# Split of the weights in pairs of K tiles, all products with the high half ahead of those with the low half, and stationary tiles on multiples of 64 bytes

## The chip, the cores and the metric

The kernel runs on one core of one Trainium2 chip. The metric is the device time of one execution in microseconds (us), the median of the runs shown. The core has five engines that run at the same time, each through its own queue in order, and wait for one another by semaphores: PE (TensorE, matmuls), DVE (VectorE), ACT (ScalarE), POOL (GpSimd) and SP (SyncE, which here only issues the loads). Weights come from HBM by DMA into SBUF; matmuls add into PSUM banks of 512 fp32 columns.

## The reference

Everything is fp32. 256 rows of 2048 columns pass through two transformer blocks. The first has an adaptive modulation (silu(c) @ w_ada, 2048 x 12288), a differential attention of 8 heads and a latent attention of 8 heads, an output projection and a squared-relu feed-forward of width 8192. The second has three attentions (sliding window, forgetting, memory) whose outputs are gated. Cut to the products that matter here:

```
mod  = silu(c) @ w_ada + b_ada                      # one row: done on DVE, not on PE
proj = modulate(rmsnorm(x)) @ w_in
x    = x + gate_m * (concat(o_diff, o_mla) @ w_out)
f    = square(relu(modulate(rmsnorm(x)) @ w_ff1)) @ w_ff2
x    = rmsnorm(x + gate_f * f)
proj = rms_norm(x) @ w_in_2                         # queries, keys, values, gates
y    = g0 * (ya @ w_a) + g1 * (yb @ w_b) + g2 * (yc @ w_c)
out  = x + y @ w_out_2
```

## The kernel before

**The products.** Every weight product is one "unit": 256 rows times K tiles of 128, into n output columns (n is 512 mostly, else 384, 320, 268 or 256). The activations are the stationary operand, 128 x 128, and the weights are the moving one, 128 x n. To keep fp32 precision each operand is split into a high half of type fp32r and a low half, the rest: for the weights `whi` is a copy of `raw` and `wlo` is `raw - whi`. Each product then is three matmuls: high times high (L324), activations high times weights low (L325), activations low times weights high (L326). A pair of K tiles needs 2 (K tiles) x 2 (row halves t) x 3 = 12 matmuls, in the order of these lines, K tile by K tile. The stationary tiles are called lhsA (attention inputs, first feed-forward product, the second block's input), lhsF (second feed-forward product), lhsM (memory), yz (branch products) and lhsY (last product); each has a `_hi` and a `_lo` half of 16,384 bytes a partition.

**The weights' way.** `plan` is the list of all loads in order, each with two K tiles (512 KB at n = 512), of kind "w" (weights for PE) or "a" and "spare" (pieces of w_ada, which DVE multiplies and adds at L493, or ACT at L491). SP loads them into `raw`, 4 slots, by `load_to` (L211); slot j % 4 is free when the split of load j-4 is done. `consume` (L221) splits one load: for each of its two K tiles one copy on ACT (L234) and one subtraction on DVE (L235), each of n columns, into one of NSPLIT = 7 slots of `whi` and `wlo`. A slot is taken again when the last matmul that reads it (L326 for t = 1) is done.

**The order.** `run` (L296) writes one unit. Ahead of the matmuls of load j, `consume_to(ahead_of(j))` puts the splits up to the second next weight load on the queues of ACT and DVE, and the pieces of w_ada between them. Then come the 12 matmuls, then `pump`, which lets the background generators in `bg` put one step each: attention heads (`causal_head`, `softmax_pv`, `diff_head`), transposes (L379), norms. So each queue holds, in turn, a split, background steps, a split, and so on. The order is fixed when the program is written; only semaphores move things in time. A background step often has work on ACT or DVE that PE waits for in the same step: in `causal_head` DVE writes `lb` (L1363), which the matmul at L1370 reads.

**The memory.** Tensors of SBUF lie one behind another in the order in which they are made, rounded to 32 bytes. `cst` has 1320 columns of 4 bytes, 5280 bytes, which is 82.5 times 64, and `vec` 173 columns, 692 bytes, rounded to 704 (11 times 64). lhsA, `raw`, `whi` and `wlo` lie ahead of `cst` and start at multiples of 64 bytes. All that is made after `cst` starts 32 bytes past one: lhsM, lhsF, yz and lhsY among it.

Of the kernel before, what the change touches and what calls it, by code (L numbers as in the profile page):

```python
# [8 lines left out]
F32 = mybir.dt.float32  # L9
F32R = mybir.dt.float32r  # L10
I32 = mybir.dt.int32
ALU = mybir.AluOpType
ACT = mybir.ActivationFunctionType
AX = mybir.AxisListType.X

P = 128
D = 2048
EPS = 1e-6
LAM0 = 0.8 - 0.6 * float(np.exp(-0.0))
NRAW, NSPLIT = 4, 7  # L20
MAGIC = 12582912.0
RSEED = float(0x5F3759DF)
TWO_PI = (6.28125, 1.93500518798828125e-3, 3.0199160510240e-7)
PI_CLAMP = 3.1415925


C_ID, C_ONE, C_U, C_REL, C_MASK, C_INV, C_END = 0, 128, 256, 512, 896, 1280, 1320

V_SHM, V_SCM, V_SHF, V_SCF, V_GM, V_GF, V_N2, V_MN = [16 * i for i in range(8)]
V_C, V_QA, V_KVA, V_SUB, V_QGA, V_KGA, V_QGB, V_KGB, V_QGC, V_KGC, V_GG, V_END = (  # L30
    128, 144, 148, 150, 151, 152, 153, 154, 155, 156, 157, 173)
# [62 lines left out]
def build(nc, ctx, a, out):  # L94
    def sb(name, shape, dt=F32, scope=ctx):
        return scope.enter_context(nc.sbuf_tensor(name, shape, dt))
# [4 lines left out]
    PE, AC, DV, PO = (Queue(sem(f"s_{n}")) for n in ("pe", "act", "dve", "pool"))  # L101
# [4 lines left out]
    lhsA = Lhs(sb("lhsA_hi", [P, 16, 256], F32R), sb("lhsA_lo", [P, 16, 256], F32R), 16)  # L106
    rows = [Bank(sb(f"row{i}", [P, 2, 512])) for i in range(3)]
    raw = sb("raw", [P, NRAW, 1024])
    whi = sb("whi", [P, NSPLIT, 512], F32R)
    wlo = sb("wlo", [P, NSPLIT, 512], F32R)  # L110
    probs = [Bank(sb(f"probs{i}", [P, 4, 256])) for i in range(2)]
    pts = [Bank(sb(f"pt{i}", [P, 512])) for i in range(2)]
    tmps = [Bank(sb(f"tmp{i}", [P, 512])) for i in range(2)]
    cst = sb("cst", [P, C_END])
    vec = sb("vec", [P, V_END])
    mods = sb("mods", [P, 64])
    small = sb("small", [P, 640])
    mkT = sb("mkT", [P, 4, 256])
# [6 lines left out]
    G = [ctx.enter_context(nc.psum_tensor(f"g{i}", [P, 512], F32)) for i in range(4)]  # L125
    gfree = [[], []]
# [81 lines left out]
    state = dict(load=0, split=0, nsplit=0, unit=0)  # L208
    landed, halves, read, side_loads = {}, {}, {}, {}
# [11 lines left out]
    def consume():  # L221

        j = state["split"]
        kind, _, n, what = plan[j]
        load_to(j + NRAW)
        src = raw[:, j % NRAW, 0:2 * n]
        if kind == "w":
            parts = []
            for kk in range(2):
                s = state["nsplit"]  # L230
                state["nsplit"] += 1
                free = read[s - NSPLIT] if s >= NSPLIT else []
                x, hi, lo = src[:, kk * n:kk * n + n], whi[:, s % NSPLIT, 0:n], wlo[:, s % NSPLIT, 0:n]
                t_hi = AC.put(lambda e, x=x, hi=hi: e.activation(hi, x, ACT.Copy), landed[j], free)  # L234
                t_lo = DV.put(lambda e, x=x, hi=hi, lo=lo: e.tensor_tensor(lo, x, hi.bitcast(F32), ALU.subtract),  # L235
                              landed[j], t_hi, free)
                parts.append((s, hi, lo, t_lo))
            halves[j] = parts
            raw_free[j % NRAW] = [t_lo]
        else:  # L240
            raw_free[j % NRAW] = [ada_part(src, landed[j], *what)]
        state["split"] += 1
        if sums_due and j >= sums_due[0][0]:
            ada_reduce(*sums_due.popleft()[1])
        load_to(j + 1 + NRAW)
# [50 lines left out]
    def run(u, steps=1, width=2):  # L296

        par = state["unit"] % 2
        state["unit"] += 1
        lhs, n, K = u["lhs"], u["n"], u["K"]  # L300
        for b in GB[2 * par:2 * par + 2]:
            while b.busy:
                pump(1, 4)
            gfree[par] = gfree[par] + b.free
            b.free = []
        for i, j in enumerate(u["tiles"]):
            while state["split"] < j and plan[state["split"]][0] == "spare":
                consume()
                pump(1, 6)
            consume_to(ahead_of(j))  # L310
            pair = u["pairs"][i] + u["k_off"] // 2
            while lhs.ready[pair] is None:
                pump(1, 3)
            for kk in range(2):
                k = 2 * i + kk
                ka = 2 * pair + kk
                s, h, l, t_lo = halves[j][kk]
                for t in range(2):
                    o = G[2 * par + t][:, 0:n]
                    xh = lhs.hi[:, ka, t * P:t * P + P]  # L320
                    xl = lhs.lo[:, ka, t * P:t * P + P]
                    first, last = k == 0, k == K - 1
                    w = [t_lo, lhs.ready[pair]] + (gfree[par] if first else [])
                    PE.put(lambda e, o=o, x=xh, w=h, f=first: e.matmul(o, x, w, start=f, stop=False), w, mark=False)  # L324
                    PE.put(lambda e, o=o, x=xh, w=l: e.matmul(o, x, w, start=False, stop=False), mark=False)  # L325
                    tok = PE.put(lambda e, o=o, x=xl, w=h, f=last: e.matmul(o, x, w, start=False, stop=f),  # L326
                                 mark=t == 1)
                read[s] = [tok]
            pump(steps, width)
        u["tok"], u["par"] = tok, par  # L330
        lhs.free = [tok]
        return par, tok
# [142 lines left out]
    start = ExitStack()  # L475
# [72 lines left out]
    k = ready_c["vec"] = t_cols  # L548
# [140 lines left out]
    par, tok = run(u_mem[0], width=3)  # L689
# [7 lines left out]
    par, tok = run(u_mem[1])  # L697
# [343 lines left out]
    for i in range(6):  # L1041
        par, tok = run(u_h0[i], width=3)
# [617 lines left out]
```

How the kernel before makes its waits and increments, by code:

```python
    def run(self, eng):  # L60
        seen = {}
        for waits, fn, sem, by in self.items:
            for s, v in waits:
                if v > seen.get(id(s), 0):
                    eng.wait_ge(s, v)
                    seen[id(s)] = v
            ins = fn(eng)
            if sem is not None:
                ins.then_inc(sem, by)
# [1516 lines left out]
    @block.sync  # L1586
    def _(eng):
        SP.run(eng)
        eng.wait_ge(*t_out)
```

## Time and profile before

| | us |
|---|---|
| median of 3 runs | 2256.26 |
| lowest and highest run | 2246.44, 2257.49 |
| profiled execution, span from first to last instruction | 2249.4 |
| PE busy in it | 2028.9 |
| DVE busy | 1452.0 |
| ACT busy | 1061.2 |
| POOL busy | 215.8 |

The profiled execution is told by its span; the profile has no time for what lies around it. Busy time is the time in which at least one instruction of the engine is in flight. Matmuls are pipelined: one of 512 columns is in flight for 0.39 us while the next has already started, so a busy PE says nothing of its pace, and the pace is read from start to start. The stages lie thus in the span: memory keys and values to 126 us, the first block's input and attention and its output projection to the first feed-forward result at 682, the feed-forward to 1405, the second block's input and attention to the first gate at 1807, gates and branches to 2154, the last product to the end. Pieces of w_ada are used among the weights up to 764 us.

### The profile page before, as it was taken

To read this page: it belongs to the slowest core of one execution; us is meant where nothing else is said; L and a number is where in the kernel's file an instruction comes from. 1 tells how busy PE (TensorE), PEld (TensorE's weight loads), DVE (VectorE), ACT (ScalarE), POOL (GpSimd) and SP (SyncE) were. 2 spreads that over 40 slices of the span, in tenths; PEclk is the share of its full clock that TensorE was granted. 3 is DMA by queue.
4 is the path that set the end of the run, shared out by engine and by line. 5 is a ranking of instruction groups with operands and counts; after the bars stand their busy time and mean duration, and the time that the engine had idled before them with its cause. 6 is when DMAs were issued, how large, how long until landed. Compare 5 with 4: busy or idle time off the path is not lost. (4 is left out here: it accounts for less than half of the span.)

```text
span 2249.4 us, 26960 instructions
## 1 busy us (share of the span) xinstructions
PE 2028.9 (90%) x9432; PEld 1673.3 (74%) x9432; DVE 1452.0 (65%) x2623; ACT 1061.2 (47%) x2120; POOL 215.8 (10%) x247
## 2 busy tenths in 40 slices
PE   5568868977869899999999999988999999999999
PEld 4456656755657688888888887977988887888877
DVE  6887787767778765555555555667666655556544
ACT  3444434553454444544544554545545454444443
POOL 0020043300100010011011012020001001001000
PEclk9788988987999999999999999998999999999999
DMA  8779877636868856555556555643554456666654
GB/s 301 239 248 295 284 262 251 229 94 220 281 234 297 270 178 199 182 189 186 188 173 202 183 181 191 195 117 106 152 148 144 121 162 200 182 196 186 189 188 158
DMA packets 239209, 450.01 MB, mean 200 GB/s; under 512 B 14304, under 2 KB 45280, under 8 KB 238432
## 3 DMA queue, kind: packets, MB, share of 16 engines
q1 hardware_dynamic: 236096, 435.84, 60.5%
q0 software_dynamic: 1856, 9.44, 1.2%
q10 hardware_dynamic: 1120, 3.01, 0.4%
q8 instruction: 74, 1.21, 0.2%
q14 instruction: 63, 0.52, 0.1%
HBM read 444.03 MB, written 4.19 MB: 199 GB/s over the span
## 5 line engine op out<-in xcount | busy, mean ns | idle before, releaser
L235 DVE TENSOR_TENSOR wlo<-raw,whi 128x512 fp32r<-128x512 f32 (+4 forms) x1336 | 896.2, 705 | 516.8 <-ACT whi L234 491.8
L234 ACT ACTIVATE whi<-raw 128x512 fp32r<-128x512 f32 (+4 forms) x1336 | 772.9, 605 | 779.0 <-PE g L326 470.8
L324 PE MATMUL g<-whi,lhsA_hi 128*128 128x512 f32 (+4 forms) x1840 | 716.3, 389 | 43.4 <-DVE wlo L235 34.3
L326 PE MATMUL g<-whi,lhsA_lo 128*128 128x512 f32 (+4 forms) x1840 | 695.0, 378 | 0.0
L325 PE MATMUL g<-wlo,lhsA_hi 128*128 128x512 f32 (+4 forms) x1840 | 694.5, 377 | 0.0
L324 PEld LDWEIGHTS g<-whi,lhsA_hi 128*128 128x128 f32 x1840 | 353.7, 192 | 116.2 <-DVE wlo L235 49.8
L326 PEld LDWEIGHTS g<-whi,lhsA_lo 128*128 128x128 f32 x1840 | 352.3, 191 | 56.9
L325 PEld LDWEIGHTS g<-wlo,lhsA_hi 128*128 128x128 f32 x1840 | 353.7, 192 | 52.4 <-issue 1.2
L493 DVE SCALAR_TENSOR_TENSOR acc<-raw,small,acc 128x512 f32<-128x512 f32 x360 | 278.7, 774 | 37.6 <-DMA raw<-in_w_ada 14.6
L324 PE MATMUL g<-whi,lhsF_hi 128*128 128x512 f32 x512 | 203.8, 398 | 1.1 <-DVE wlo L235 1.1
L325 PE MATMUL g<-wlo,lhsF_hi 128*128 128x512 f32 x512 | 202.2, 395 | 0.0
L326 PE MATMUL g<-whi,lhsF_lo 128*128 128x512 f32 x512 | 202.1, 395 | 0.0
L1113 POOL TENSOR_TENSOR region<-region,tmp 128x512 f32<-128x512 f32 x40 | 57.0, 1444 | 770.4 <-DVE tmp L1109 759.5
L324 PEld LDWEIGHTS g<-whi,lhsF_hi 128*128 128x128 f32 x512 | 96.0, 187 | 24.5 <-DVE wlo L235 1.5
L326 PEld LDWEIGHTS g<-whi,lhsF_lo 128*128 128x128 f32 x512 | 96.0, 187 | 23.5
L325 PEld LDWEIGHTS g<-wlo,lhsF_hi 128*128 128x128 f32 x512 | 96.0, 188 | 23.0 <-issue 0.2
L762 POOL TENSOR_TENSOR rot<-row,trig 128x64 f32<-128x64 f32 (+1 forms) x72 | 37.7, 552 | 231.0 <-ACT row L387 186.3
L517 PE MATMUL pT<-cst,acc 128*128 128x1 f32 x128 | 21.8, 291 | 37.5 <-DVE acc L493 37.5
L1109 DVE TENSOR_TENSOR tmp<-g,region 128x512 f32<-128x512 f32 x40 | 25.8, 686 | 45.9 <-PE g L326 45.9
L517 PEld LDWEIGHTS pT<-cst,acc 128*128 128x128 f32 x128 | 21.6, 251 | 41.5 <-DVE acc L493 40.4
L324 PE MATMUL g<-whi,lhsY_hi 128*128 128x512 f32 x128 | 51.1, 399 | 0.0
L324 PE MATMUL g<-whi,lhsM_hi 128*128 128x512 f32 x64 | 32.0, 501 | 20.9 <-DVE wlo L235 11.5
(291 smaller groups left out, 1690.2 us busy)
## 6 DMA issues: line engine op xcount, KB each, us to landing
raw<-in_w_ff SPq DMA_DIRECT2D x256, 512.0 KB, 4.3
raw<-in_w_ada SPq DMA_DIRECT2D x192, 512.0 KB, 4.8
raw<-in_w_in SPq DMA_DIRECT2D x176, 512.0 KB, 4.4
raw<-in_w_out SPq DMA_DIRECT2D x64, 512.0 KB, 4.7
raw<-in_w_in SPq DMA_DIRECT2D x80, 384.0 KB, 3.6
raw<-in_w_mem_kv SPq DMA_DIRECT2D x16, 512.0 KB, 5.4
raw<-in_w_branch_a SPq DMA_DIRECT2D x12, 512.0 KB, 4.1
raw<-in_w_branch_b SPq DMA_DIRECT2D x12, 512.0 KB, 3.9
```

Source lines behind the costliest of these rows:

```text
L234: t_hi = AC.put(lambda e, x=x, hi=hi: e.activation(hi, x, ACT.Copy), landed[j], free)
L235: t_lo = DV.put(lambda e, x=x, hi=hi, lo=lo: e.tensor_tensor(lo, x, hi.bitcast(F32), ALU.subtract), landed[j], t_hi, free)
L324: PE.put(lambda e, o=o, x=xh, w=h, f=first: e.matmul(o, x, w, start=f, stop=False), w, mark=False)
L325: PE.put(lambda e, o=o, x=xh, w=l: e.matmul(o, x, w, start=False, stop=False), mark=False)
L326: tok = PE.put(lambda e, o=o, x=xl, w=h, f=last: e.matmul(o, x, w, start=False, stop=f), mark=t == 1)
L493: t = DV.put(lambda e, w=w, s=s: e.scalar_tensor_tensor(out=o, in0=w, scalar=s, in1=o, op0=ALU.mult, op1=ALU.add), t_in, b.tok)
L517: tok = PE.put(lambda e, m=m: e.matmul(T.ap[:, m:m + 1], b.ap[:, P * m:P * m + P], ones[:, 0:1], start=True, stop=True), b.tok, T.free, t_cst)
L762: ks = [PO.put(lambda e, o=o, i0=i0, i1=i1: e.tensor_tensor(o, i0, i1, ALU.mult), *w) for o, i0, i1 in ((r[0], u, cos), (r[1], v, sin), (r ...
L1109: k = DV.put(lambda e, t=t, tm=tm: e.tensor_tensor(tm.ap[:, :], G[2 * par + t][:, :], g[:, 512 * j:512 * j + 512], ALU.mult), tok, tm.free ...
L1113: k = PO.put(lambda e, xc=xc, tm=tm: e.tensor_tensor(xc, xc, tm.ap[:, :], ALU.add), k, x_tok[j])
```

## The change

`cst` becomes 1328 columns (5312 bytes, 83 times 64) and `vec` is made with 176, of which 173 are used, so every tensor starts at a multiple of 64 bytes. `consume` makes one copy on ACT and one subtraction on DVE for both K tiles of a load, 2n columns wide. `whi` and `wlo` get 3 slots of 1024 columns in place of 7 of 512 (12,288 bytes a partition each in place of 14,336). In `run` the 12 matmuls of a load come in two rounds: first for each K tile and row half the two that read `whi` (activations high, then low), waiting for the copy alone, and then the four that read `wlo`, waiting for the subtraction. One slot is given back per load, after the last matmul, and the bit that ends an accumulation moves from the low-activation product to the last one with `wlo`. The number of matmuls, their shapes, the loads and the background work stay as they were.

```diff
-NRAW, NSPLIT = 4, 7
+NRAW, NSPLIT = 4, 3
-C_ID, C_ONE, C_U, C_REL, C_MASK, C_INV, C_END = 0, 128, 256, 512, 896, 1280, 1320
+C_ID, C_ONE, C_U, C_REL, C_MASK, C_INV, C_END = 0, 128, 256, 512, 896, 1280, 1328
-    whi = sb("whi", [P, NSPLIT, 512], F32R)
-    wlo = sb("wlo", [P, NSPLIT, 512], F32R)
+    whi = sb("whi", [P, NSPLIT, 1024], F32R)
+    wlo = sb("wlo", [P, NSPLIT, 1024], F32R)
-    vec = sb("vec", [P, V_END])
+    vec = sb("vec", [P, 176])[:, 0:V_END]
@@ consume
-            parts = []
-            for kk in range(2):
-                s = state["nsplit"]
-                state["nsplit"] += 1
-                free = read[s - NSPLIT] if s >= NSPLIT else []
-                x, hi, lo = src[:, kk * n:kk * n + n], whi[:, s % NSPLIT, 0:n], wlo[:, s % NSPLIT, 0:n]
-                t_hi = AC.put(lambda e, x=x, hi=hi: e.activation(hi, x, ACT.Copy), landed[j], free)
-                t_lo = DV.put(lambda e, x=x, hi=hi, lo=lo: e.tensor_tensor(lo, x, hi.bitcast(F32), ALU.subtract),
-                              landed[j], t_hi, free)
-                parts.append((s, hi, lo, t_lo))
-            halves[j] = parts
+            s = state["nsplit"]
+            state["nsplit"] += 1
+            free = read[s - NSPLIT] if s >= NSPLIT else []
+            hi, lo = whi[:, s % NSPLIT, 0:2 * n], wlo[:, s % NSPLIT, 0:2 * n]
+            t_hi = AC.put(lambda e: e.activation(hi, src, ACT.Copy), landed[j], free)
+            t_lo = DV.put(lambda e: e.tensor_tensor(lo, src, hi.bitcast(F32), ALU.subtract), landed[j], t_hi, free)
+            halves[j] = (s, hi, lo, t_hi, t_lo)
             raw_free[j % NRAW] = [t_lo]
@@ run
-            for kk in range(2):
-                k = 2 * i + kk
-                ka = 2 * pair + kk
-                s, h, l, t_lo = halves[j][kk]
-                for t in range(2):
...
-                    w = [t_lo, lhs.ready[pair]] + (gfree[par] if first else [])
-                    PE.put(lambda e, o=o, x=xh, w=h, f=first: e.matmul(o, x, w, start=f, stop=False), w, mark=False)
-                    PE.put(lambda e, o=o, x=xh, w=l: e.matmul(o, x, w, start=False, stop=False), mark=False)
-                    tok = PE.put(lambda e, o=o, x=xl, w=h, f=last: e.matmul(o, x, w, start=False, stop=f),
-                                 mark=t == 1)
-                read[s] = [tok]
+            s, hi, lo, t_hi, t_lo = halves[j]
+            steps_of = [(kk, t) for kk in range(2) for t in range(2)]
+            end = i == len(u["tiles"]) - 1
+            for kk, t in steps_of:
+                o, h = G[2 * par + t][:, 0:n], hi[:, kk * n:kk * n + n]
...
+                w = [t_hi, lhs.ready[pair]] + (gfree[par] if first else [])
+                PE.put(lambda e, o=o, x=xh, w=h, f=first: e.matmul(o, x, w, start=f, stop=False), w, mark=False)
+                PE.put(lambda e, o=o, x=xl, w=h: e.matmul(o, x, w, start=False, stop=False), mark=False)
+            for kk, t in steps_of:
+                o, l = G[2 * par + t][:, 0:n], lo[:, kk * n:kk * n + n]
...
+                tok = PE.put(lambda e, o=o, x=xh, w=l, f=end and kk == 1: e.matmul(o, x, w, start=False, stop=f), t_lo,
+                             mark=kk == t == 1)
+            read[s] = [tok]
```

## Rows read from the trace of the kernel before

**Rows 1.** The page: busy us by engine, and PE's busy tenths in 40 slices.

```profile
PE 2028.9 (90%) x9432; PEld 1673.3 (74%) x9432; DVE 1452.0 (65%) x2623; ACT 1061.2 (47%) x2120; POOL 215.8 (10%) x247
...
PE   5568868977869899999999999988999999999999
```

**Rows 2.** Windows: length, busy us (x) of PE, PEld, DVE, ACT, POOL, clock, DMA.

```profile
2155.90:2244.45 88.55, 88.55 (x381) 71.04 (x379) 44.09 (x67) 36.77 (x59) 1.44 (x2) 1.00 0.55 184
130.00:300.00 170.00, 137.59 (x610) 109.41 (x610) 134.29 (x228) 73.76 (x142) 5.61 (x13) 0.94 0.87 285
520.00:800.00 280.00, 239.37 (x1031) 188.94 (x1031) 209.78 (x338) 126.10 (x236) 15.83 (x13) 0.94 0.78 263
...
1800.00:2245.00 445.00, 436.99 (x1935) 356.54 (x1933) 241.72 (x373) 208.58 (x359) 26.25 (x20) 1.00 0.58 183
```

**Rows 3.** Timeline of PE: start us, duration us, line, operands.

```profile
1137.70 0.39 PE L325 MATMUL g<-wlo,lhsF_hi 128*128 128x512 f32 x1
...
1217.96 0.40 PE L324 MATMUL g<-whi,lhsF_hi 128*128 128x512 f32 x1
1218.19 0.39 PE L325 MATMUL g<-wlo,lhsF_hi 128*128 128x512 f32 x1
1218.42 0.39 PE L326 MATMUL g<-whi,lhsF_lo 128*128 128x512 f32 x1
1218.65 0.39 PE L324 MATMUL g<-whi,lhsA_hi 128*128 128x512 f32 x1
...
1242.90 0.39 PE L326 MATMUL g<-whi,lhsA_lo 128*128 128x512 f32 x1
```

**Rows 4.** Groups by line, 130 to 300 us: busy, mean ns, idle before, ended by.

```profile
L234 ACT ACTIVATE whi<-raw 128x512 fp32r<-128x512 f32 x72 | 41.5, 623 | 78.0 <-DMA raw<-in_w_in 77.9
```

**Rows 5.** DMA issues, 130 to 300 us: count, KB, median us to landing.

```profile
raw<-in_w_ada SPq DMA_DIRECT2D x51, 512.0 KB, 4.8
```

**Rows 6.** Groups by line and shape, whole span, columns as in rows 4.

```profile
L324 PE MATMUL g<-whi,lhsA_hi 128*128 128x512 f32 x1360 | 552.1, 406 | 39.2 <-DVE wlo L235 30.2 <-DVE lhsA_lo L726 8.7
...
L324 PE MATMUL g<-whi,lhsF_hi 128*128 128x512 f32 x512 | 203.8, 398 | 1.1 <-DVE wlo L235 1.1
...
L324 PE MATMUL g<-whi,lhsY_hi 128*128 128x512 f32 x128 | 51.1, 399 | 0.0
...
L324 PE MATMUL g<-whi,yz_hi 128*128 128x512 f32 x128 | 50.6, 395 | 0.0
...
L324 PE MATMUL g<-whi,lhsM_hi 128*128 128x512 f32 x64 | 32.0, 501 | 20.9 <-DVE wlo L235 11.5 <-DVE lhsM_lo L370 9.4
...
L626 ACT ACTIVATE hn_sq<-region 128x1024 f32<-128x1024 f32 x8 | 8.5, 1058 | 2.5 <-DVE small L664 2.2
```

**Rows 7.** Timeline of splits of 512 columns (x2: two merged).

```profile
212.18 1.15 ACT L234 ACTIVATE whi<-raw 128x512 fp32r<-128x512 f32 x2 [2.83 <-DMA raw<-in_w_in]
...
213.22 1.29 DVE L235 TENSOR_TENSOR wlo<-raw,whi 128x512 fp32r<-128x512 f32 x2
...
1004.12 0.69 DVE L235 TENSOR_TENSOR wlo<-raw,whi 128x512 fp32r<-128x512 f32 x1 [0.59 <-ACT whi L234]
```

**Rows 8.** Timeline of one step with 384 columns in the forgetting attention.

```profile
1687.05 0.53 ACT L234 ACTIVATE whi<-raw 128x384 fp32r<-128x384 f32 x1 [3.40 <-PE g L326]
...
1687.49 0.48 DVE L1363 TENSOR_SCALAR lb<-cst,small 128x128 f32<-128x128 f32 x2
...
1687.88 1.02 DVE L235 TENSOR_TENSOR wlo<-raw,whi 128x384 fp32r<-128x384 f32 x2
...
1688.40 0.49 PE L1370 MATMUL pS<-cst,lb 128*128 128x128 f32 x2
```

**Rows 9.** The page: costliest groups (all shapes) and DMA issues.

```profile
L235 DVE TENSOR_TENSOR wlo<-raw,whi 128x512 fp32r<-128x512 f32 (+4 forms) x1336 | 896.2, 705 | 516.8 <-ACT whi L234 491.8
...
raw<-in_w_ff SPq DMA_DIRECT2D x256, 512.0 KB, 4.3
```

**Rows 10.** Waits, 800 to 1400 us: us in total, times, longest us.

```profile
ACT whi L234 <- PE g L326: 219.0, 308, 1.1
```

More of the change, by code:

```diff
@@ L313, in run @@
                 pump(1, 3)
-            for kk in range(2):
-                k = 2 * i + kk
-                ka = 2 * pair + kk
-                s, h, l, t_lo = halves[j][kk]
-                for t in range(2):
[L319 to L322, printed above, removed]
-                    w = [t_lo, lhs.ready[pair]] + (gfree[par] if first else [])
-                    PE.put(lambda e, o=o, x=xh, w=h, f=first: e.matmul(o, x, w, start=f, stop=False), w, mark=False)
-                    PE.put(lambda e, o=o, x=xh, w=l: e.matmul(o, x, w, start=False, stop=False), mark=False)
-                    tok = PE.put(lambda e, o=o, x=xl, w=h, f=last: e.matmul(o, x, w, start=False, stop=f),
-                                 mark=t == 1)
-                read[s] = [tok]
+            s, hi, lo, t_hi, t_lo = halves[j]
[3 more added lines that the diff above has]
+                o, h = G[2 * par + t][:, 0:n], hi[:, kk * n:kk * n + n]
+                xh = lhs.hi[:, 2 * pair + kk, t * P:t * P + P]
+                xl = lhs.lo[:, 2 * pair + kk, t * P:t * P + P]
+                first = i == 0 and kk == 0
+                w = [t_hi, lhs.ready[pair]] + (gfree[par] if first else [])
[3 more added lines that the diff above has]
+                o, l = G[2 * par + t][:, 0:n], lo[:, kk * n:kk * n + n]
+                xh = lhs.hi[:, 2 * pair + kk, t * P:t * P + P]
+                tok = PE.put(lambda e, o=o, x=xh, w=l, f=end and kk == 1: e.matmul(o, x, w, start=False, stop=f), t_lo,
+                             mark=kk == t == 1)
+            read[s] = [tok]
             pump(steps, width)
```

## The prediction

> **What bounds the kernel now.** I began with the page's busy times by engine and its slices [rows 1]. TensorE has matmuls in flight in 90% of the 2249.4 us. From slice 15 on its digits are nearly all 9; in the first 14, some 790 us, they lie between 5 and 9 with a mean near 7. So there are two regimes, and the windows separate them [rows 2]. From 1800 to 2245 us PE is busy 437.0 of 445 us, at full clock. From 130 to 300 us it is only 137.6 of 170, DVE is busy 134.3, the granted clock is 0.94, and the DMA engines are 87% busy at 285 GB/s; 520 to 800 us is a milder form, at 78% and 263 GB/s.
>
> The late regime is a stream of products, so what counts is the distance from one matmul to the next. Durations mislead here (0.39 us each, and they overlap), so I took start times from the timeline [rows 3]. Between 1137.70 and 1218.42 us 347 matmuls with lhsF as stationary operand start without a break: 80.72/346 = 233.3 ns. The next ones read lhsA: 108 of them from 1218.65 to 1242.90, 24.25/107 = 226.6 ns. Lines, moving tiles, the 512 columns and the clock are the same; the stationary tile differs. lhsA lies at a multiple of 64 bytes. lhsF, lhsM, lhsY and yz lie behind cst (5280 bytes, 82.5 times 64) and so 32 bytes off. lhsY, at another place than lhsF, shows the same: 380 products in 88.55 us, 233 ns [rows 2].
>
> In the early regime I asked who waits. From 130 to 300 us ACT's copy into whi sat idle 78.0 us for the raw tile to land [rows 4], and a load itself waits for a free raw slot, which the subtraction on DVE gives back. That is a loop: four slots, 4.8 us from issue to landing [rows 5]. 512 KB at 285 GB/s are a load in 1.84 us, so a slot comes round in 7.36 us, of which 2.5 are ACT, DVE and their queues.
>
> **The change, part by part.** The sum is made against the profiled execution, 2249.4 us of span; the profile shows no time around it. The median of the runs is 6.9 us above that (2256.3), the lowest run 3 us below. I carry differences over to the median unchanged. What a measurement of this kernel can tell from no change is about 0.5%, 11 us.
>
> *Alignment (C_END, vec).* Products whose stationary tile is 32 bytes off: [rows 6] per line 512 with lhsF, 128 with lhsY, 128 with yz, 64 with lhsM; times three lines 1536 + 384 + 384 + 192 = 2496. All but lhsM's 192 run where PE hardly waits. 2304 x 6.7 ns = 15 us off. Bounds: 0, if the 6.7 ns belong to something other than the start address, and 17 with lhsM. I take 15.
>
> *Width of the split.* ACT: two copies now take 1.15 us together [rows 7]; one of 1024 columns should take 1.06, as L626's, the same engine and width [rows 6]. DVE: two subtractions take 1.29 together, one 0.69; two of 384 columns take 1.02 [rows 8], so a column costs 0.27/256 = 1.05 ns and 1024 cost 1.23 us. Saved per pair of K tiles: 0.09 and 0.06 us, over 1336/2 = 668 pairs [rows 9] 60 us of ACT and 40 of DVE, almost all of it beside matmuls. What reaches the end is between 0 and some 5 us (chains of attention and norms, where PE waits for ACT or DVE); I take 2.
>
> The trace has the second subtraction start 0.60 us after the first although each lasts 0.69 [rows 7]: the two overlap a little. The Trainium skill, Advanced Engine Details and Errata, section The Read-Write Bubble, says that memory accesses are not pipelined from one instruction to the next, and VectorE: DVE Perf Modes, section on the TRN2 errata, gives (N+151)/0.96 ns for this operation, 691 for 512 columns and 1224 for 1024. The durations agree with the trace; the missing overlap does not. By the pages DVE would save 0.16 us a pair, 105 us in all; with DVE not the bound past 800 us this would not move the sum by more than the 5 us above.
>
> *High half first.* PE now waits for t_lo before any product of a K tile: 0.63 + 0.69 + two handovers of 0.05, 1.4 us from landing. Afterwards the first eight products need only t_hi: 1.06 + 0.05. So PE starts 0.3 us sooner on a tile it was waiting for, and the low half, 1.28 us later, arrives while eight products (1.8 us) run: no second wait follows. What it touches is PE's idle time behind L235, 30.2 + 1.1 + 11.5 = 43 us [rows 6]. Most of it stands in the loop stretch, where PE is not in the loop and the next landing sets the pace. I take 4 off; bounds 0 and 20, half of the 43. The order itself I cost at nothing: L326 to the next L324 changes the PSUM bank and the stationary tile, L324 to L325 changes neither, and both stand 0.23 us apart [rows 3].
>
> *A raw slot is held longer.* It is freed by the end of the whole subtraction: now 0.63 + 0.05 + 1.29 = 2.0 us after landing, afterwards 1.06 + 0.05 + 1.23 = 2.35. About half the loads there are weights; the ada load behind one on DVE is put off by 0 to 0.35. The mean is some 0.27 us longer on 7.36, 3.7%, if landing takes as long as before. But it takes 4.3 us where loads are sparse (w_ff) and 4.8 where they are dense [rows 5, 9], so fewer in flight give back perhaps half: 1.6%. The stretches at the loop are 170 us and about half of 280, 310 in all: 5 us. Bounds: 0 and 12.
>
> *Three slots of two K tiles for seven of one.* The first copy for tiles j+2 waited for the products of j-2, the second for half of those of j-1; now the one copy waits for all of j-1. Is it in time? Copy and subtraction end 2.35 us after products j start, and are needed at j+2, 5.4 us after. In the feed-forward part ACT already waits for PE before its copies (308 times, 219.0 us [rows 10]): it is ahead, and a longer wait costs nothing directly. Queued behind the waiting copy, though, is the background work of ACT and DVE, and PE waits for that. [Rows 8] show the narrow case, 384 columns: the copy starts at 1687.05 with half the products done, DVE's lb is ready at 1687.97, PE reads it at 1688.40, slack 0.4 us. With the copy held half a tile longer (6 x 0.17 = 1.0 us), and one of twice the length in front, DVE's background starts up to 1.3 us later: PE would wait 0.9 us. At each of 12 heads of that form, 11 us; but several come in steps with more slack. I take 4; bounds 0 and 11.
>
> Sum: -15 - 2 - 4 + 5 + 4 = -12 us; 2256.3 - 12 = 2244 us.
>
> **Rivals.**
> (a) *The raw loop decides.* Place: the whole early part, 0 to 450 and 520 to 800 us, 730 us. Price: 0.36 us a turn, if each subtraction puts off the ada load behind it in full and landing does not shorten: 0.36/7.36 = 4.9%, 36 us. With -15 - 2 - 4 + 4 that is +19, 2275 us. It decides once more than 350 us run at that price. For: ACT starved in 78.0 of 170 us, DMA at 87%. Against: at 87% the DMA engines, not the slots, carry most of the time.
> (b) *The 6.7 ns are not the start address* but the tile's place in the memory. Then this edit does not do what it says: -2 - 4 + 9 = +3, 2259 us. For: all off-line tiles lie behind lhsA. Against: lhsF and lhsY lie at two places and show one distance.
> (c) *The early part loosens up.* PE's waits for wlo fall by the full 20 us, the chains by 5, the attention loses nothing: -15 - 5 - 20 + 5 = -35, 2221 us. For: 31 us of such waits outside lhsM. Against: the loop.
> (d) *The distance falls to the array's own time.* 512 columns at 2.4 GHz are 213 ns, and aligned tiles show 227. If the rest came from the order high, low, high, with one tile loaded twice running, the three quarters of 668 x 12 products that run past 800 us would each give back up to 13 ns: 78 us with the forecast's 12, 2166 us. Against: L324 to L325 (the same stationary tile) and L326 to L324 (another) stand equally far apart [rows 3].
> The Trainium skill, TensorE: Matmul & The Clock Gate, section Back-to-back issue gap, has N/2.4 + 2.5 ns, 216 for 512 columns; the trace has 227 and 233, so by that rule (d) is what there would be to win.
>
> **How the numbers follow.** Forecast 0.52 (own range 2236 to 2252), (a) 0.10, (b) 0.14, (c) 0.21, (d) 0.03. Range 2227 to 2260: it leaves out (d), nearly all of (a) and the lower end of (c). Faster than 2245: somewhat over half of the forecast's case, all of (c) and (d), 0.52. Slower than 2267: (a) and a tail of (b), 0.10. Within: 0.38.
>
> **What would show it.** Alignment: lhsF's products start 227 ns apart instead of 233. Width: L234 and L235 each 668 times, about 1.06 and 1.23 us. High first: PE's idle time before L324 is no longer ended by L235 but by L234, and is less. Loop: the loads of 130 to 300 us take up to 5 us more, below 285 GB/s. Slots: waits of L1370 for L1363 appear between 1660 and 1800 us. The prediction is wrong if lhsF's distance stays at 233, if the first 800 us move by more than 10 us either way, or if PE waits for L234 past 800 us.

## The result, and the profile after

The changed kernel takes 2270.2 us (median of 4 runs, 2261.4 to 2276.1) against 2253.5 for the kernel before (2246.4 to 2257.5): ratio 1.0069, 95% interval 1.0043 to 1.0095. It is slower by 17 us where 12 less were forecast, outside the range, and nearest to rival (a). The profiled execution is the fastest of the four: span 2259.6 us against 2249.4, so the two traces account for 10 of the 17 us. The kernel before was timed again beside each group of experiments, at 2253.4 to 2254.4 us, so times of different groups may be compared. In the other three runs the mean granted clock is 0.948 to 0.951 against 0.955 in the profiled one; what put it there is not in the trace.

The page of the changed kernel (busy us by engine; PE's busy tenths in 40 slices; costliest groups: busy, mean ns, idle before, ended by), against [rows 1, 9]:

```profile
PE 2018.9 (89%) x9432; PEld 1674.9 (74%) x9432; DVE 1367.2 (61%) x1955; ACT 966.5 (43%) x1452; POOL 235.7 (10%) x247
...
PE   5567877976869899999999999988999999999999
...
L233 DVE TENSOR_TENSOR wlo<-raw,whi 128x1024 fp32r<-128x1024 f32 (+3 forms) x668 | 806.3, 1209 | 750.1 <-ACT whi L232 733.3
L232 ACT ACTIVATE whi<-raw 128x1024 fp32r<-128x1024 f32 (+3 forms) x668 | 675.3, 1012 | 1029.1 <-PE g L324 734.1
...
L1111 POOL TENSOR_TENSOR region<-region,tmp 128x512 f32<-128x512 f32 x40 | 63.3, 1603 | 758.2 <-DVE tmp L1107 749.1
...
raw<-in_w_ff SPq DMA_DIRECT2D x256, 512.0 KB, 4.2
raw<-in_w_ada SPq DMA_DIRECT2D x192, 512.0 KB, 4.8
```

The splits became what they were to become: 668 of each, 85 us less of DVE and 95 less of ACT. And that bought nothing. DVE's idle time ended by the copy has gone from 491.8 us [rows 9] to 733.3: busy time has turned into waiting in front of the same step.

Windows of the changed kernel, columns as in [rows 2]:

```profile
130.00:300.00 170.00, 134.81 (x593) 108.50 (x594) 125.47 (x173) 68.16 (x96) 5.41 (x13) 0.92 0.86 275
520.00:800.00 280.00, 230.28 (x972) 179.74 (x973) 202.93 (x271) 112.97 (x157) 12.81 (x11) 0.91 0.77 257
1800.00:2245.00 445.00, 434.53 (x1954) 358.99 (x1953) 227.94 (x235) 189.27 (x223) 29.99 (x20) 1.00 0.63 187
```

In both early windows it starts fewer matmuls (593 for 610, 972 for 1031), at 275 for 285 and 257 for 263 GB/s and a lower clock. Groups by line, 130 to 300 us, against [rows 4]:

```profile
L232 ACT ACTIVATE whi<-raw 128x1024 fp32r<-128x1024 f32 (+1 forms) x42 | 41.8, 997 | 95.3 <-DMA raw<-in_w_in 90.0 <-PE g L324 5.3
```

ACT waits 90.0 us for landings instead of 77.9. In the late window PE starts 1954 matmuls for 1935, in 434.5 busy us for 437.0. The spacing of the lhsF products comes from a window that begins with the first and ends with the last start of an unbroken stretch:

```profile
791.24:869.72 78.48, 78.48 (x348) 64.94 (x347) 42.62 (x37) 30.83 (x30) 10.60 (x6) 1.00 0.61 191
```

347 matmuls start in it (the 348th began just ahead of it): 78.48/346 = 226.8 ns, where [rows 3] gave 233.3. PE's idle time by line and shape, against [rows 6]:

```profile
L319 PE MATMUL g<-whi,lhsA_hi 128*128 128x512 f32 x1360 | 554.6, 408 | 41.3 <-ACT whi L232 29.6 <-DVE lhsA_lo L724 11.6
```

It was 39.2, of which 30.2 behind the subtraction; it is 41.3, of which 29.6 behind the copy. PE waits for another instruction, and as long.

**One table for all kernels.** Each pair of K tiles has 12 products, so the start of product 12j in the timeline of PE says when pair j began. Pairs 156, 384 and 540 of the 668 bound four parts: the loads' part; the feed-forward part, where PE runs without a break; the attention part, with background work; the end. Lengths in us, from the profiled executions (median: all timed runs; that of the kernel before as timed beside the first group; the last column ends at the last product's start, so the four don't add up to the span; hold: median us from a weight tile's landing to the start of the load that takes its raw slot, pairs 24 to 60):

```
                      hold  0-156  156-384  384-540  540-667   median of runs
before                2.07  766.4   652.2    460.3    365.5    2253.8
after                 2.42  780.9   643.0    468.0    362.7    2270.2
a1_align_only         2.07  771.1   642.9    459.7    362.3    2243.1
a2_narrow_six         2.07  767.8   641.7    459.0    362.2    2237.6
a3_raw5               2.43  738.9   643.0    470.8    362.4    2223.6
a4_wide_old_order     2.43  786.0   642.8    469.3    362.4    2270.7
b3_after_unaligned    2.42  783.4   653.6    471.4    367.1    2282.7
c1_narrow_raw5        2.09  722.7   642.0    459.2    362.1    2192.9
c3_two_subtractions   2.49  780.7   645.5    469.2    361.0    2269.7
d1_before_raw5        2.08  722.6   651.2    462.2    365.5    2208.0
e1_two_copies         2.52  794.3   644.5    471.7    362.7    2276.3
e2_halves_joined      2.07  766.3   645.5    461.1    359.5    2240.8
e3_own_waits          2.07  766.3   641.8    459.9    359.5    2239.2
b2_align_six_raw5     2.09  722.1   642.9    459.8    362.0    2193.8
f1_late_release       2.27  774.1   644.1    461.5    361.1    2252.0
f2_raw3_slots4        2.42  895.1   644.0    469.5    362.7    2377.7
f3_sub_later          2.43  785.6   645.8    458.0    361.1    2254.3
f4_mixed_raw5         2.07  723.6   643.1    468.0    362.6    2207.3
```

After less before: +14.5, -9.2, +7.7, -2.8. The alignment gave 12 of its 15 us in the second and fourth part, and two losses lie in the first and third. A single length of the first part is good to some 5 us: with four raw slots the five kernels whose hold is 2.07 have 766.3 to 771.1 (a1, which only aligns, the 771.1), the five of 2.42 to 2.49 have 780.7 to 786.0. The groups are clearly apart, by 16 us in the mean.

### The profile page after: what moved, and what is told of

It is laid out like the page before. It is cut to its first block and busy times, and to the rows that moved or that the text cites. A ratio compares the mean times of both kernels' runs of the same rounds, so it can differ in the third digit from the quotient of the medians.

```text
span 2259.6 us, 25164 instructions
## 1 busy us (share of the span) xinstructions
PE 2018.9 (89%) x9432; PEld 1674.9 (74%) x9432; DVE 1367.2 (61%) x1955; ACT 966.5 (43%) x1452; POOL 235.7 (10%) x247
## 3 DMA queue, kind: packets, MB, share of 16 engines
q8 instruction: 74, 1.21, 0.2%
## 5 line engine op out<-in xcount | busy, mean ns | idle before, releaser
L233 DVE TENSOR_TENSOR wlo<-raw,whi 128x1024 fp32r<-128x1024 f32 (+3 forms) x668 | 806.3, 1209 | 750.1 <-ACT whi L232 733.3
L232 ACT ACTIVATE whi<-raw 128x1024 fp32r<-128x1024 f32 (+3 forms) x668 | 675.3, 1012 | 1029.1 <-PE g L324 734.1
L324 PE MATMUL g<-wlo,lhsA_hi 128*128 128x512 f32 (+4 forms) x1840 | 468.2, 377 | 1.8 <-DVE wlo L233 1.7
L324 PEld LDWEIGHTS g<-wlo,lhsA_hi 128*128 128x128 f32 x1840 | 342.4, 192 | 59.0 <-DVE wlo L233 3.2
L491 DVE SCALAR_TENSOR_TENSOR acc<-raw,small,acc 128x512 f32<-128x512 f32 x360 | 281.6, 782 | 34.3 <-DMA raw<-in_w_ada 17.1
L1111 POOL TENSOR_TENSOR region<-region,tmp 128x512 f32<-128x512 f32 x40 | 63.3, 1603 | 758.2 <-DVE tmp L1107 749.1
L324 PE MATMUL g<-wlo,lhsF_hi 128*128 128x512 f32 x512 | 136.9, 389 | 0.0
L320 PEld LDWEIGHTS g<-whi,lhsF_lo 128*128 128x128 f32 x512 | 96.2, 188 | 19.9 <-issue 0.2
L1559 POOL TENSOR_TENSOR y<-y,tmp 128x512 f32<-128x512 f32 x16 | 27.1, 1713 | 264.4 <-DVE tmp L1553 264.4
L659 POOL TENSOR_TENSOR hn_sq<-row 128x384 f32<-128x384 f32 (+2 forms) x18 | 19.5, 1105 | 302.7 <-ACT row L385 302.7
```

Of the source, the lines that this page charges most:

```text
L232: t_hi = AC.put(lambda e: e.activation(hi, src, ACT.Copy), landed[j], free)
L233: t_lo = DV.put(lambda e: e.tensor_tensor(lo, src, hi.bitcast(F32), ALU.subtract), landed[j], t_hi, free)
L320: PE.put(lambda e, o=o, x=xl, w=h: e.matmul(o, x, w, start=False, stop=False), mark=False)
L324: tok = PE.put(lambda e, o=o, x=xh, w=l, f=end and kk == 1: e.matmul(o, x, w, start=False, stop=f), t_lo, mark=kk == t == 1)
L491: t = DV.put(lambda e, w=w, s=s: e.scalar_tensor_tensor(out=o, in0=w, scalar=s, in1=o, op0=ALU.mult, op1=ALU.add), t_in, b.tok)
L1111: k = PO.put(lambda e, xc=xc, tm=tm: e.tensor_tensor(xc, xc, tm.ap[:, :], ALU.add), k, x_tok[j])
```

## First group: which of the four edits

My theory was rival (a): the wider split holds the raw slot longer, in the loop of the loads. Rivals: the address, the later reuse of the split slots, the order of the products.

a1, from the kernel before (the diffs of this and the next sections are in short form where a loop is rewritten):

```diff
-C_INV, C_END = 1280, 1320
+C_INV, C_END = 1280, 1328
-vec = sb("vec", [P, V_END])
+vec = sb("vec", [P, 176])[:, 0:V_END]
```

> The kernel before with cst of 1328 and vec of 176 columns, nothing else. Address theory: lhsF's, lhsY's and yz's products stand 227 ns apart and the time is 2253.5 - 15 = 2238 us. If the address only helps together with the new order, the distance stays at 233 and the time at 2253.

Measured 2243.1, ratio 0.9948 (0.9929 to 0.9967): 10.7 us less where 15 were expected, in the trace all of it behind pair 156, and the products of lhsF stand 227 ns apart. a2, a1 with the high half first and six split slots, two narrow splits a pair as before:

```diff
-NRAW, NSPLIT = 4, 7
+NRAW, NSPLIT = 4, 6
+for kk, t: w = [t_hi of kk, ...]; high.whi, low.whi
+for kk, t: high.wlo, t_lo of kk; read[s of kk] = [tok]
```

> The changed kernel with the split made again in two copies and two subtractions of n columns (6 slots of 512 for whi and wlo, the same memory as 3 of 1024); order high first, alignment and the late release of the slots as in the changed one. Width theory (a raw slot or GpSimd is held up by the longer instructions): the lost 25 us of the other edits come back, 2240 us. Slot theory (ACT and DVE are let go later, since a load's slots come free only after its last product): it stays near 2265.

Measured 2237.6, ratio 0.9933 (0.9911 to 0.9954). All that is left between it and the changed kernel is the width and what is joined with it, and that is 33 us. The slots' theory falls. a3, from the changed kernel:

```diff
-NRAW, NSPLIT = 4, 3
+NRAW, NSPLIT = 5, 3
```

> The changed kernel with 5 raw slots in place of 4. Loop theory (a raw slot is held longer, and the loads wait for it): the first 800 us win back their 14 us and more, 2250 us or less. If the loss is in the chains of background work instead: no change beyond 5 us, 2265 us, with the DMA engines as busy as before.

Measured 2223.6, ratio 0.9865 (0.9846 to 0.9884): 46 us below the changed kernel, 42 of them before pair 156. a4: the changed kernel with its wide splits and the old order, which waits for the low half:

```diff
-  w = [t_hi, ...]; high.whi, low.whi for all four; then high.wlo with t_lo
+  w = [t_lo, ...]; for kk, t: high.whi, high.wlo, low.whi
```

> The changed kernel with the products in the old order (high, weights low, activations low), each load's first product waiting for the subtraction; wide split, 3 slots and alignment kept. If the order is worth what the prediction took, it is 4 us slower than the changed kernel (2274); if PE's start plays no part, equal to it (2270); if the new order itself is the loss, near 2245.

Measured 2270.7, ratio 1.0072 (1.0054 to 1.0090). With wide splits the order is worth nothing that can be told. Between a1 and a2 stand 5.6 us with overlapping intervals; those two differ in the split slots too.

## Second group: does the fifth slot cure the width

c1, from a2:

```diff
-NRAW, NSPLIT = 4, 6
+NRAW, NSPLIT = 5, 6
```

> Narrow split (two copies and two subtractions of 512), high half first, aligned, six split slots, and five raw slots instead of four; to be read against 2237.6 (same with four) and 2223.6 (changed kernel with five). Theory A, the wide split cost its 33 us only by holding a raw slot longer: with a fifth slot the loads no longer wait for it, the width is worth little, and this ends within 6 us of the wide one, 2218 to 2227. Theory B, the wide instructions cost by themselves (they lengthen the GpSimd operations and the chains between the tiles): the 33 us stay, 2187 to 2200. Theory C, the fifth slot cures only what the wide split spoiled and is worth nothing to a narrow one: 2234 to 2241.

Measured 2192.9, ratio 0.9732 (0.9717 to 0.9748). That is in the window of theory B, and against my theory A as I had put it: the fifth slot gives the narrow kernel 45 us and the wide one 46, and 31 us lie between them as before. c3, from the changed kernel, then asks whether it is the long DVE instruction:

```diff
-  t_lo = DV.put(subtract, lo, src, hi)                 # 1024 columns
+  for kk in range(2): t_lo = DV.put(subtract, lo[kk], src[kk], hi[kk])
```

> The changed kernel with the wide copy on ScalarE kept and the subtraction made in two of 512, the slot still released by the last. Theory A, the hold of the raw slot from landing to the last subtraction decides: 1.01 + 0.69 + 0.60 is not shorter than 1.01 + 1.21, so this is as slow as the changed kernel, 2264 to 2277. Theory B, the 1.21 us VectorE instruction decides (GpSimd operations of 1.60 us beside it instead of 1.44): the GpSimd mean falls back under 1.5 us and the time to 2237 to 2248.

Measured 2269.7, ratio 1.0071 (1.0055 to 1.0086). Groups of its GpSimd operations (busy, mean ns):

```profile
L1114 POOL TENSOR_TENSOR region<-region,tmp 128x512 f32<-128x512 f32 x40 | 56.8, 1441 | 771.4 <-DVE tmp L1110 762.9 <-DMA region<-in_x 8.5
...
L1562 POOL TENSOR_TENSOR y<-y,tmp 128x512 f32<-128x512 f32 x16 | 23.3, 1478 | 266.5 <-DVE tmp L1556 266.5
```

GpSimd is back from 1603 to 1441 ns, and the time has not moved. Theory B falls. d1 (from the kernel before) and b3 (from the changed kernel):

```diff
 d1:
-NRAW, NSPLIT = 4, 7
+NRAW, NSPLIT = 5, 6
 b3:
-C_INV, C_END = 1280, 1328
+C_INV, C_END = 1280, 1320
-vec = sb("vec", [P, 176])[:, 0:V_END]
+vec = sb("vec", [P, V_END])
```

> The kernel before with five raw slots and six split slots, nothing else changed (old order, narrow, stationary operands 32 bytes off). Theory A, the loop of loads cost the kernel before something as well: it gains what the narrow kernel gains from the fifth slot, about 15 us, 2235 to 2243. Theory C, the kernel before was not held by its raw slots: 2250 to 2257.

Measured 2208.0, ratio 0.9797 (0.9782 to 0.9811): the kernel before was held by its raw slots as much as any, 44 us before pair 156 (its split slots go from seven to six along with it). I had expected a third of that.

> The changed kernel with the constants and the vectors at their old widths, so that the stationary operands lie 32 bytes off a multiple of 64 again. Alignment theory, terms add up: 2270 + 11 = 2281, range 2276 to 2288, and the distance of products in the lhsF stretch is 233.3 ns again. Rival, in the wide kernel the loads decide so often that TensorE's pace is covered: 2268 to 2274, with the distance at 233.3 ns all the same. Rival on the address: the distance stays 226.8 ns and the cause is the order or the width.

Measured 2282.7, ratio 1.0124 (1.0107 to 1.0142); 12.5 us above the changed kernel. One unbroken lhsF stretch of it:

```profile
795.44:876.17 80.73, 80.73 (x348) 64.85 (x346) 42.45 (x37) 30.87 (x30) 10.60 (x6) 1.00 0.59 186
```

80.73/346 = 233.3 ns. Rival (b) is out: with wide splits and the new order too, 32 bytes of start address make the difference.

## Third group: length of the chain, or joined waits

e1 splits only the copy; e2 copy and subtraction, the first subtraction beside the second copy; e3 as e2, each product with the wait of its own half.

```diff
 e1: for kk in range(2): t_hi = AC.put(copy of half kk)     # subtraction of 1024 kept
 e2: for kk in range(2):
         t_hi = AC.put(copy of half kk)
         t_lo = DV.put(subtraction of half kk, t_hi)        # products wait for the last
 e3: ... w = [t_hi[kk], ...]  and  t_lo[kk]
```

> The changed kernel with the copy on ScalarE made in two of 512 (the products and the subtraction wait for the second), the subtraction kept at 1024. Copy theory, the 1.01 us copy on ScalarE is what costs: back to 2237 to 2247. Hold theory, what counts is the stretch from landing to the last subtraction, which stays as long (about 2 x 0.6 + 1.21): 2266 to 2276.

> The changed kernel with two copies and two subtractions of 512, the first subtraction beside the second copy; the products still wait for both halves and the slot is reused when both are read. The hold from landing to the last subtraction shrinks from 1.01 + 1.21 to about 0.60 + 0.60 + 0.69 us. Hold theory: most of the 33 us are gone, 2237 to 2247. Joined-wait theory, that a pair of tiles goes through waits and slots as one is what costs, whatever the width: 2262 to 2274.

> As the one before, and each product waits for the copy or the subtraction of its own half; only the reuse of the slot is still for the pair of tiles. It differs from the 2237.6 us kernel by that alone. Hold theory: 2236 to 2246, as the one before. Joined waits of the products: the one before slow, this one 2237 to 2247. Joined reuse of the slot (the copies of tile pair j wait for the last product of j-3 instead of its first half's, 0.45 us later): both slow, over 2260.

Measured: e1 2276.3, ratio 1.0094 (1.0073 to 1.0115); e2 2240.8, 0.9947 (0.9928 to 0.9966); e3 2239.2, 0.9932 (0.9915 to 0.9949). Splitting either instruction alone does nothing; splitting both, so that they overlap, brings 29 us back, and the joined waits cost nothing that can be told (1.6 us between e2 and e3). What counts is the length of the chain copy-subtraction. The timeline of the changed kernel shows it (start us, us; in brackets the idle time before and what ended it; x2: two merged):

```profile
204.01 1.06 ACT L232 ACTIVATE whi<-raw 128x1024 fp32r<-128x1024 f32 x1 [3.07 <-DMA raw<-in_w_in]
...
205.16 1.23 DVE L233 TENSOR_TENSOR wlo<-raw,whi 128x1024 fp32r<-128x1024 f32 x1 [0.89 <-ACT whi L232]
...
206.41 0.37 SPq L54 DMA_DIRECT2D raw<-in_w_ada  x1
```

and that of e2:

```profile
200.87 1.16 ACT L235 ACTIVATE whi<-raw 128x512 fp32r<-128x512 f32 x2 [2.51 <-DMA raw<-in_w_in]
...
201.59 1.29 DVE L236 TENSOR_TENSOR wlo<-raw,whi 128x512 fp32r<-128x512 f32 x2 [0.43 <-ACT whi L235]
...
202.91 0.37 SPq L54 DMA_DIRECT2D raw<-in_w_ada  x1
```

The tile has landed, ACT starts, and the load that takes its slot is issued 2.40 us later in the one and 2.04 in the other, although both instructions of e2 take longer in sum: its DVE starts after 0.72 us instead of 1.15. b2: d1 with the edit of a1.

> The kernel before with five raw slots, six split slots and the stationary operands at multiples of 64 bytes, old order of the products. Against 2208.0 (the same unaligned) the alignment gives its 11: 2197; against 2192.9 (the same with the high half first) the order is worth the difference. Order theory (worth 4 us, as the 4 us between a1 and a2 hint): 2195 to 2200. Order worth nothing, as in the wide kernel: 2191 to 2195.

Measured 2193.8, ratio 0.9737 (0.9715 to 0.9758): the alignment gives 14 us here, and the order again nothing that can be told (c1: 2192.9).

## Fourth group: two places, two ways

The chain costs in the first part and in the third, and a fifth raw slot leaves the third as it is (470.8 us for 459.2 without the width). f1 is e2 with the slot released one small GpSimd instruction later:

```diff
+  if s < 156:
+      t_lo = PO.put(memset(pause[:, 0:64], 0.0), t_lo)     # halves[j] keeps the old token
   raw_free[j % NRAW] = [t_lo]
```

> The kernel with both halves overlapping (2240.8), and for the first 156 pairs of tiles the raw slot is released one small GpSimd instruction after the last subtraction, some 0.3 to 0.5 us later; no other engine waits for it. Hold theory: 14 us came for 0.3 us of hold, so the first 156 pairs end 12 to 24 us later, and nothing changes behind them: 2252 to 2266. Queue theory (VectorE stands behind the long copy, the hold itself is harmless): 2238 to 2245.

Measured 2252.0, ratio 0.9993 (0.9983 to 1.0003), 11 us above e2. That is at the lower edge of the hold theory's window, clear of the queue theory's. The hold grew by 0.20 us, less than I had thought (the memset takes 0.15), and the first part by 7.8 us where 12 to 24 were expected; GpSimd's own work waited 0.7 us for it. So the hold alone costs. The changed kernel, with 0.35 us more than e2, lost 14.6. (There is no exact law: e1, with a hold 0.10 longer than the changed kernel's, loses 13 us more.)

The traces say where the time went. A raw slot is always either waiting for its load to land or held, so a quarter of the sum of both over loads 8 to 345 is the time that these loads take. The table gives the quarter sums in us (a hold counts here also where the tile waits for ACT or DVE to come to it):

```
                 time    landing  hold of weights  hold of ada pieces
before           735.4   418.5    124.1            193.1
after            749.3   419.5    132.5            197.6
e2_halves_joined 734.5   420.3    123.5            191.0
f1_late_release  742.8   418.8    132.5            191.7
```

Landing hardly moves. f1 and the changed kernel hold a weight tile longer than e2 by the same 0.24 us in the mean of these loads (the 0.35 is the median, and 0.22 the mean against the kernel before). What the changed kernel pays beyond f1 stands in the slots of the ada pieces, which queue behind the long subtraction on DVE: their median hold is 2.59 us for 2.31 in the kernel before.

f2 is the changed kernel with `NRAW, NSPLIT = 3, 4`:

> The changed kernel with three raw slots and four wide split slots. Read in two parts. Before pair 156 the hold theory wants the loop of 7.3 us shared by three: 50 to 80 us more. Between pairs 384 and 540, where the changed kernel loses 7.7 us to the kernel before: if ScalarE's waits for a split slot are the cause, that goes to between -2 and +2; if VectorE's queue behind the long copy is, it stays at +6 to +11. In all about 2320 to 2350.

Measured 2377.7, ratio 1.0540 (1.0526 to 1.0554): 114 us more in the first part where I expected 50 to 80, and the third stays at 469.5. A further split slot doesn't cure it. f3 puts the wide subtraction into DVE's queue at the next split, behind a step of background work:

```diff
-  t_lo = DV.put(subtract ...); raw_free[j % NRAW] = [t_lo]
+  owed.append(...)        # put at the start of the next consume()
```

> The changed kernel with the wide subtraction put into VectorE's queue one step of background work later, so that VectorE does not stand waiting for the long copy; the raw slot is held longer for it. Queue theory: the loss of 7.7 us between pairs 384 and 540 goes to between -2 and +3. Hold theory: before pair 156 it is later than the changed kernel by 5 to 30 us. Both hold: 2265 to 2290. Queue theory alone (both places are VectorE's queue): 2240 to 2255.

Measured 2254.3, ratio 1.0002 (0.9989 to 1.0015). By the time alone that is the window of "queue theory alone" (2240 to 2255), and not that of both (2265 to 2290). By the parts, the third falls to 458.0, as the queue theory has it. The first is 4.7 us longer than the changed kernel's, just short of the 5 that the hold theory asked and inside the scatter (a4 has 786.0), and nothing of its loss came back, which speaks against the queue there. The waits of the third part, in the kernel before (us in total, times, longest):

```profile
DVE wlo L235 <- ACT whi L234: 97.2, 99, 4.9
...
PE pT L379 <- POOL row L670: 10.4, 5, 4.1
```

in the changed kernel:

```profile
DVE wlo L233 <- ACT whi L232: 167.9, 114, 4.6
...
PE pT L377 <- POOL row L668: 14.4, 5, 5.2
```

in f3:

```profile
DVE wlo L227 <- ACT whi L243: 85.2, 59, 3.1
...
PE pT L389 <- POOL row L680: 6.6, 5, 1.6
```

and in c3, whose third part is as long as the changed kernel's:

```profile
DVE wlo L235 <- ACT whi L232: 150.6, 102, 4.3
...
PE pT L380 <- POOL row L671: 10.6, 5, 4.4
```

Against the changed kernel, f3's DVE stands half as long behind the copy, and PE's wait for the norms that GpSimd finishes falls by 8 us. But these two waits are not the whole path: e2, which has no such loss, has 143.9 and 10.6 us of them, nearly c3's. PE's whole idle time in the third part is 23.2 us in the kernel before, 28.9 in the changed one, 24.7 in e2, 27.5 in c3 and 19.9 in f3, and the time at the lower of the two clocks (1.2 GHz) 17.1, 20.5, 17.1, 27.3 and 20.5. In c3 products of 512 columns start 427 ns apart at that clock and 227 at the full one. The idle time and half of the time at the lower clock, each less that of the kernel before, add up to 7.4 us (changed), 1.5 (e2), 9.4 (c3) and -1.6 (f3); the lengths differ by 7.7, 0.8, 8.9 and -2.3. So the long chain reaches the end here by idle time of PE, and in c3 for more than half by the clock. That the place in DVE's queue is the link is what f3 suggests; since f3 also gains over the kernel before, it may in part make good another loss. f4, from a3:

```diff
+if s < 156:     # the halves of e2
+    ...
+else:           # the wide copy and subtraction
```

> Halves overlapping for the first 156 pairs, the wide split of the changed kernel behind them, five raw slots. If the two losses are separate places: 2192.9 + 8 to 12 for pairs 384 to 540 = 2200 to 2206. If the wide split costs through something that both parts share (clock, GpSimd, all the products), it is nearer the middle of 2192.9 and 2223.6 or above: 2207 to 2220.

Measured 2207.3, ratio 0.9791 (0.9777 to 0.9805), 14.4 above c1. The median lies at the lower edge of the second theory's window, the parts don't fit it: 723.6 us (c1 722.7) and 468.0 (c1 459.2), the rest the same to 1.6. The two losses are separate places; the trace accounts for 11.3 of the 14.4 us.

The best versions are c1 and b2 at 2193 and 2194 us, 2.7% below the kernel before: aligned, narrow splits, six split slots, five raw slots. They differ in the order of the products alone.

## Why the prediction was wrong

- *What bounds it*: right, and too weakly held. There is the loop of raw slots before 800 us, and it decided there by far more than I allowed: one slot more is worth 44 us to the kernel before.
- *Alignment, -15*: right in the mechanism, and 1 to 4 us too high. The spacing fell to 226.8 ns; three pairs of kernels differ by 10.7 (a1), 12.5 (b3) and 14.2 us (b2).
- *Width, -2*: the durations were right (1.06 and 1.23 us in the timeline). The busy time saved was more than worked out, 98 us of the copies and 90 of the subtractions for 60 and 40. The rows I used were short ones: over all 548 loads of 512 columns the subtractions took 1.40 us a load before, for the 1.29 of the row (one of them 733 ns in the mean, for 0.69 us), and 1.26 after; the copies 1.21 and 1.06. None of it came to the end. The Trainium skill, Advanced Engine Details and Errata, section The Read-Write Bubble, led with the formula beside it in the prediction to 105 us of DVE; the 90 are nearer to that than to my 40. That does not bear out the page's reason: in 425 of the 668 loads of the kernel before, the second subtraction starts before the first has ended.
- *High half first, -4*: not shown. 0.6 us between a4 and the changed kernel, 0.9 between b2 and c1, and at most part of the 5.6 between a1 and a2. PE's idle time ended by the split did change its name from L235 to L232, as the list of signs said, and kept its size. Rival (c) lived on such gains and is out with it, and (d) by the 226.8 ns, which the new order left as they were.
- *Raw slot held longer, +5*: **this step failed.** The hold itself was right: 2.0 to 2.35 us forecast, 2.07 to 2.42 measured. Wrong were the two discounts on it. The larger is "fewer in flight give back perhaps half". They gave nothing: from pair 24 to 60 a load took 4.78 us in the mean to land before and 4.88 after, and in the sums above landing makes +1.0 of 13.9 us. The smaller let the ada loads escape part of the delay, 0.27 for 0.35 over all loads; the median hold of the ada slots rose by 0.28 us, and they make 4.5 of the 13.9. Without discounts 310 us at 7.36 a turn are 42 turns, and 42 turns of 0.35 us are 14.7, for 14.5 measured. That they meet so closely is in part luck: the first stretch, 130 to 300 us, lost about 4 us where its turns give 8, and 4 more were lost outside both stretches (against the kernel before, the changed one starts later by 2.0 us at pair 16, 6.0 at 60, 7.9 at 96, 14.5 at 156). A sign I had named came true: the first 800 us moved by more than 10. I had read the 4.3 us of the feed-forward loads as what fewer in flight give back; a hold longer by 5% of a turn hardly changes their number. The right value lay above my bound of 12.
- *Slots and background, +4*: place and bound right (7.7 us, bound 11), mechanism wrong. I let the reuse of the slot delay what is queued behind it. The sign I had named, L1370 behind L1363, stayed at 1.4 us (0.8 before). A fourth slot changes nothing (f2), joined slots with a short chain cost 0.8 (e2). The long chain does it; that it does so through DVE's place in line behind the long copy is likely (f3), and not shown by itself.
- *Rival (a)* had the direction, at 0.10 far too small a chance. "DMA at 87%, not the slots, carries most of the time" was the argument against it. With a fifth slot the same engines reach 92%:

```profile
130.00:300.00 170.00, 147.88 (x662) 121.25 (x660) 144.63 (x247) 76.03 (x146) 16.17 (x32) 0.91 0.92 309
```

This is c1: 309 GB/s for 285 [rows 2], 662 matmuls for 610. 87% was no wall. The time came out 5 us under (a)'s, and that is in part luck: (a) had the 36 us over 730 us of loads, and the loads' part lost 14.5.

In one sum for the profiled executions: -12 forecast, +10.2 measured. Of the 22 us between them the raw slot makes 9.5, the background 3.7, width and order 6, and the alignment 3 (12.0 in the second and fourth part, for 15). Open stays why the medians differ by 17 us and the two traces by 10, and with it why f3 is 16 us below the changed kernel by the medians and 4 by the traces.

## What to carry to other kernels

Halving the number of instructions saves busy time and lengthens each link of a chain: where copy and subtraction of a tile run on two engines, two halves that overlap free the buffer sooner (2.07 us) than one wide pair of less busy time (2.42). Before such an edit ask for each buffer how long it is held and how many turns wait for it, price the turns in full, and try one slot more first. A queue in front of a wait is a cost of its own: the same wide subtraction, put one step later in the queue, gave back 10 us in one part (in all, its trace is 4 us shorter than the changed kernel's).

## What the runs showed of the hardware

- A float32r stationary operand that starts 32 bytes off a multiple of 64 costs 6.5 ns a matmul of 512 columns (233.3 against 226.8 ns), with the new order of products (233.3 in b3, 226.8 in the changed kernel) as with the old (233.3 in the kernel before and d1, 227.0 in a1 in the mean of all its 1503 unbroken steps with lhsF). The order of the products changes neither figure.
- GpSimd operations of 512 columns took 1443 ns where the subtractions had 512 columns (a1) and 1603 where they had 1024 (the changed kernel, and e1 with its narrow copies); with the subtraction in two (c3) it was 1441, and the kernel's time did not move.
- Load time grows with the slots, and far less than the slots gain: with three, four and five slots the wide kernel's loads of pairs 24 to 60 took 4.44, 4.88 and 5.20 us to land in the mean, and its first part 895.1, 780.9 and 738.9 us.
